# Second layer's output projection as fourteen half-size products instead of 128 full tile products

## The chip, the cores and the metric

The kernel runs on one core of one Trainium2 chip. The metric is the device time of one execution in microseconds. Three runs of the kernel before gave 971.11, 971.8 and 973.08 us, so the median is 971.8 us. The program is bound to one core, and the whole network (two layers) is one launch.

## The reference

512 tokens with 1024 features pass two layers. Each layer does: RMSNorm, a mixer, `h += RMSNorm(mixer output)`, and then a gated embedding (`ple`): `h += sigmoid(RMSNorm(h) W_g) * (p W_p)`. The mixer of layer 0 is a convolution and a gMLP; that of layer 1 is an mLSTM with 8 heads in 4 chunks of 128 tokens. Both mixers end in an output projection:

```
def mlstm_mixer(xn, w_in, b_if, mh_g, w_out):
    q, k, v, o, z, gif = jnp.split(xn @ w_in, ODD_SPLITS, axis=-1)
    ...                                   # hc: (512, 2048), 8 heads of 256
    y = hc * jax.nn.sigmoid(o) * jax.nn.silu(z)
    return y @ w_out                      # (512, 2048) @ (2048, 1024)

h = h + rmsnorm(y, post_g[i])
gate = jax.nn.sigmoid(rmsnorm(h, ple_g[i]) @ w_ple_gate[i])
h = h + gate * (p[i] @ w_ple[i])
```

All is float32. The change is about `y @ w_out` of layer 1.

## The kernel before

**Number format.** Every float32 operand of a large product is split in two float32r parts, `hi` (a copy by ScalarE) and `lo` (the original minus `hi`, by VectorE). A product is three matmuls: hi by hi, hi by lo, lo by hi. So each weight block costs ScalarE two activations and VectorE two subtractions of 128x1024, and each left operand is split likewise.

**Seven products for eight.** A product of two matrices cut in 2x2 blocks is done in seven block products instead of eight, with sums and differences of blocks on both sides (a Strassen scheme in Winograd's form). The products of a unit are named 1, 5, 6, 3, 2, 7, 4. Left sums are made by VectorE, right (weight) sums by a DMA that adds into SBUF (issued by GpSimd, `add_in`, `out_add`) or by VectorE (`s6_add`). One product has two passes `tp` (row tiles), each of 4 contraction tiles with 3 matmuls of 512 columns, so 12 matmuls a pass and 24 a product. The result gathers in PSUM banks: `a_of`, `b_of`, `c_of` are banks 0/1, 2/3, 4/5; small intermediate sums (`b_copy`, `s5_copy`, `c_make`) stand between products.

**Order of the work.** The input projections are 15 units (0 to 6 in layer 0, 7 to 14 in layer 1), each of seven products, in the list `STEPS`. Layer 0's output projection is already in this list, as 2 x 7 products (two halves `h` of the contraction) in the order `OUT_ORDER`. Each engine has its order written out by hand; semaphores join them. A weight block passes: SP loads it into one of five raw buffers (`raw7`: BX, BV, BA, BY, BZ), GpSimd may add another block to it there, ScalarE (`hi7`, L877) and VectorE (`lo7`, L1576) split it into a ring of three slots, TensorE uses it. The split of step g+2 is done during step g.

**Layer 1's output projection before.** It is a plain product (`odd_out` of TensorE, `token_tile` with L2331 to L2333): 2 column halves x 4 weight slots x 4 token tiles x 4 contraction tiles x 3 = 384 matmuls of 512 columns. The left operand y is split tile by tile (`y_high` L1037, `y_low` L1779), the first twelve tiles during the last input unit (unit 14), the last four (heads 6 and 7) during the projection. Weight slots are split by `hi` (L814) and `lo` (L1541).

**Heads 6 and 7.** The mLSTM work of the last two heads is cut in pieces which TensorE does between passes of the projection (`odd_end(i)` after pass i): intermediate states (`dstate` L2724), `scores` (L2733), `head_tile` (L2742, L2746), and the transposes of finished heads (`transpose_head` L2753), which ScalarE copies to y (`y_copy` L1377). Before, they stand at i = 0, 1, 2, 3, 5, 6, 7, 8 and 10.

**The end.** After the projection come the post norm (`residual` L1886, L1890), eight `ple` tiles with the transposes of the normed h between them (L2367), and the gate projection with its outputs. Layer 0 has the same with its own order (`PLE_ORDER[0]`).

Of the kernel before, what the change touches and what calls it, by code (L numbers as in the profile page):

```python
# [25 lines left out]
F32 = mybir.dt.float32  # L26
# [4 lines left out]
P = 128  # L31
SEQ = 512
# [32 lines left out]
OUT = 20  # L65
OUT_ORDER = ((0, 1), (1, 1), (0, 2), (0, 5), (1, 2), (1, 5), (0, 6), (1, 6), (0, 3), (1, 3), (0, 7), (1, 7),
# [6 lines left out]
OUT_PLACE = {what: place for place, users in OUT_PLACES.items() for what in users}  # L73
# [5 lines left out]
STEPS += [(u, p) for u in range(LEAD, UNITS) for p in order(u)]  # L79
STEP = {what: g for g, what in enumerate(STEPS)}  # L80
# [6 lines left out]
def out_left_count(h, p):  # L87
    return OUT_LEFTS.index((h, p)) + 1


def out_sum_count(h, p):
    return OUT_SUMS.index((h, p)) + 1
# [23 lines left out]
def source(u, p):  # L116

    if u >= OUT:
        return {5: (BZ, BV), 6: (BZ, BV), 4: (BZ, BV), 2: (BX, BX), 7: (BA, BX)}.get(p, (BA, BY))[u - OUT]
# [19 lines left out]
S_OUT = [0, 5]  # L139
S_PLE = [0, 13]  # L140
S_GATE = [1, 14]
SLOTS = 18
TAIL_ROWS = ROWS_IN + 8


N_OUT = [0, 16]
N_PLE = [0, 24]
N_GATE = [8, 32]


def raw_of(s):

    l = int(s >= S_OUT[1])
    r = (s - S_OUT[l]) % 2
    return r, (s - S_OUT[l]) // 2 + 1 + (3 - r if l else 0)


SLOT_RING = (1, 2)
SPARE_RING = 0


def slot_ring(s):
    return s % RING if s < S_OUT[1] else SLOT_RING[raw_of(s)[0]]


def slot_ends():
# [12 lines left out]
    def tail(l):  # L179
        for nb in range(2 * l):  # L180
            for _ in range(3):
                half()
            full(N_OUT[l] + 4 * nb + 4)
        full(N_PLE[l] + 8)
        for nb in range(2):
            half()
            full(N_GATE[l] + 4 * nb + 4)
# [18 lines left out]
def trunk(nc, x, p_in, slots, gif_w, g_rows, ln_rows, w_mix, b_mix, conv_w, gate_bias, head_g, out):  # L206
# [3 lines left out]
    def region(at, *spec):  # L210
# [53 lines left out]
    y0_hi, = region(L_AT, ("y0_hi", [P, 14, SEQ], F32R))  # L264
    y0_lo, = region(L_AT + 28 * KB, ("y0_lo", [P, 14, SEQ], F32R))
    y0_hi_end, = region(L_AT + 56 * KB, ("y0_hi_end", [P, 2, SEQ], F32R))
# [4 lines left out]
    p_hi_odd, p_odd, tanh_g, gated, g_post, g_ple = region(  # L271
        R_AT, ("p_hi_odd", [P, 2, SEQ], F32R), ("p_odd", [P, 2, SEQ], F32),
        ("tanh_g", [P, 2, SEQ], F32), ("gated", [P, 2, SEQ], F32), ("g_post", [P, D], F32),
        ("g_ple", [P, D], F32))
    p_lo_odd, y0_lo_end = region(W_AT + 8 * KB * SPARE_RING, ("p_lo_odd", [P, 2, SEQ], F32R),
# [2719 lines left out]
```

## Time and profile before

| what | value |
|---|---|
| median of three runs | 971.8 us |
| the profiled execution, own time | 971.55 us |
| its span (first to last instruction) | 969.8 us |
| TensorE busy | 961.0 us, 99% |
| VectorE busy | 670.7 us, 69% |
| ScalarE busy | 524.7 us, 54% |
| GpSimd busy | 102.3 us, 11% |
| mean DMA rate | 169 GB/s |

The page has busy time per engine, the span in 40 slices, the DMA queues, the chain of work that ended last, and the costliest groups of instructions by source line. A timeline row gives start, duration, engine, line, operation, output<-inputs, count, and in brackets how long the engine was idle before it and what released it. Matmuls are pipelined: their durations overlap, so their cost is the distance of their starts.

### The profile page before, as it was taken

How to read it: one execution, taken by the hardware profiler on the slowest of the kernel's cores; microseconds unless marked ns; L12 is line 12 of the kernel's file. 1: busy time of each engine (PE TensorE's matmuls, PEld its weight loads, DVE VectorE, ACT ScalarE, POOL GpSimd, SP SyncE). 2: the span in 40 equal slices, each digit the busy share in tenths (PEclk: the TensorE clock that was granted, in tenths of full speed). 3: DMA queues.
4: the chain of work that ended last, by engine and by line, in shares of the span. 5: the costliest groups of instructions: out<-in, count | busy, mean ns of one | idle time of the engine just before them, and what ended most of it. 6: DMA issues, size and time to landing. Idle time of an engine off the chain costs nothing.

```text
span 969.8 us, 12032 instructions
## 1 busy us (share of the span) xinstructions
PE 961.0 (99%) x4470; PEld 795.1 (82%) x4470; DVE 670.7 (69%) x885; ACT 524.7 (54%) x839; POOL 102.3 (11%) x136
## 2 busy tenths in 40 slices
PE   8999999999999999999999999999999999999998
PEld 7888888888877888887888888888888888888887
DVE  6767787786888687749797755775585676431835
ACT  6454554555455475636665656546654774441732
POOL 2020100101000113104010101010101000000500
PEclk9999999999999999999999999999999999999999
DMA  9655947649486993745956738392938163242122
GB/s 342 201 152 152 253 153 201 174 134 273 127 227 195 253 229 131 233 115 131 323 154 175 181 123 209 106 239 98 247 108 210 30 172 125 98 162 87 44 87 88
DMA packets 26268, 163.50 MB, mean 169 GB/s; under 512 B 3297, under 2 KB 3681, under 8 KB 8418
## 3 DMA queue, kind: packets, MB, share of 16 engines
q1 hardware_dynamic: 18722, 108.20, 29.3%
q0 software_dynamic: 7488, 54.53, 29.0%
q8 instruction: 36, 0.59, 0.2%
q14 instruction: 22, 0.18, 0.1%
HBM read 158.53 MB, written 4.19 MB: 168 GB/s over the span
## 4 chain that ended last, share of the span: by engine, by line
PE 96%; DVE 1%; ACT 1%; DMA 1%; issue 0%; POOL 0%; SPq 0%; DVEq 0%; ACTq 0%
PE bank L2425 18%; PE bank L2428 18%; PE bank L2427 18%; PE bank L2331 6%; PE bank L2333 6%; PE bank L2332 6%; PE bank L2458 3%; PE bank L2461 3%; PE bank L2460 3%; PE bank L2482 2%; PE bank L2484 2%; PE bank L2483 1%; PE bank L2742 1%; PE bank L2724 1%; PE bank L2746 1%; PE bank L2367 1%
## 5 line engine op out<-in xcount | busy, mean ns | idle before, releaser
L1576 DVE TENSOR_TENSOR w_lo<-raw,w_hi 128x1024 fp32r<-128x1024 f32 x230 | 271.3, 1221 | 151.4 <-ACT w_hi L877 150.8
L2425 PE MATMUL bank<-w_hi,l_hi 128*128 128x512 f32 x784 | 316.5, 404 | 0.5 <-DVE s L1694 0.4
L2428 PE MATMUL bank<-w_hi,l_lo 128*128 128x512 f32 x784 | 305.9, 390 | 0.0
L2427 PE MATMUL bank<-w_lo,l_hi 128*128 128x512 f32 x784 | 305.5, 390 | 0.0
L877 ACT ACTIVATE w_hi<-raw 128x1024 fp32r<-128x1024 f32 x230 | 230.7, 1054 | 106.4 <-DMA raw<-in_slots 53.9
L2425 PEld LDWEIGHTS bank<-w_hi,l_hi 128*128 128x128 f32 x784 | 147.3, 188 | 33.1 <-DVE s L1694 2.1
L2428 PEld LDWEIGHTS bank<-w_hi,l_lo 128*128 128x128 f32 x784 | 147.2, 188 | 31.3
L2427 PEld LDWEIGHTS bank<-w_lo,l_hi 128*128 128x128 f32 x784 | 147.3, 188 | 30.3 <-issue 1.0
L702 POOL DMA_DIRECT2D raw<-in_slots x44 | 39.2, 972 | 461.3 <-DVE w_lo L1576 434.9
L1541 DVE TENSOR_TENSOR w_lo<-raw,w_hi 128x1024 fp32r<-128x1024 f32 x36 | 42.4, 1220 | 55.9 <-ACT w_hi L814 55.9
L814 ACT ACTIVATE w_hi<-raw 128x1024 fp32r<-128x1024 f32 x36 | 36.2, 1059 | 65.3 <-PE bank L2333 62.8
L2331 PE MATMUL bank<-w_hi,x_hi 128*128 128x512 f32 x120 | 47.0, 391 | 0.0
L2333 PE MATMUL bank<-w_hi,x_lo 128*128 128x512 f32 x120 | 46.7, 389 | 0.0
L2332 PE MATMUL bank<-w_lo,x_hi 128*128 128x512 f32 x120 | 46.7, 389 | 0.0
L2331 PE MATMUL bank<-w_hi,y_hi 128*128 128x512 f32 x112 | 44.9, 401 | 0.2 <-DVE y_lo_end L1779 0.2
L2458 PE MATMUL bank<-w_hi,l_hi 128*128 128x512 f32 x112 | 45.1, 403 | 0.0
L2333 PE MATMUL bank<-w_hi,y_lo 128*128 128x512 f32 x112 | 43.7, 390 | 0.0
L2461 PE MATMUL bank<-w_hi,l_lo 128*128 128x512 f32 x112 | 43.7, 390 | 0.0
L2332 PE MATMUL bank<-w_lo,y_hi 128*128 128x512 f32 x112 | 43.6, 390 | 0.0
L2460 PE MATMUL bank<-w_lo,l_hi 128*128 128x512 f32 x112 | 43.6, 389 | 0.0
L686 POOL TENSOR_SCALAR rstds<-sums 128x1 f32<-128x1 f32 x20 | 19.2, 958 | 112.5 <-ACT square L825 112.1
L1583 DVE TENSOR_TENSOR raw<-raw 128x1024 f32<-128x1024 f32 x26 | 30.6, 1219 | 0.0
(263 smaller groups left out, 1339.1 us busy)
## 6 DMA issues: line engine op xcount, KB each, us to landing
raw<-in_slots SPq DMA_DIRECT2D x87, 1024.0 KB, 6.8
raw<-in_slots POOLq DMA_DIRECT2D x52, 1024.0 KB, 9.0
h<-in_x SPq DMA_DIRECT2D x8, 512.0 KB, 7.1
out<-h SPq DMA_DIRECT2D x4, 512.0 KB, 7.5
h<-out SPq DMA_DIRECT2D x4, 512.0 KB, 7.7
out<-h SPq DMA_DIRECT2D x7, 256.0 KB, 2.0
raw<-in_slots SPq DMA_DIRECT2D x2, 512.0 KB, 6.1
g_post<-in_g_rows SPq DMA_DIRECT2D x2, 512.0 KB, 6.0
```

The lines of the kernel that those rows point to most:

```text
L877: act.activation(w7_hi[:, ring(g), c], raw7[:, source(u, p), c], ACT.Copy).then_inc(w7_hi_ready, 1)
L1541: dve.tensor_tensor(w7_lo[:, slot_ring(s), c], raw[:, r, c], w7_hi[:, slot_ring(s), c].bitcast(F32), ALU.subtract).then_inc(lo_ready, 1)
L1576: dve.tensor_tensor(w7_lo[:, ring(g), c], raw7[:, source(*STEPS[g]), c], w7_hi[:, ring(g), c].bitcast(F32), ALU.subtract).then_inc(w7_lo_r ...
L2331: pe.matmul(bank[b][:, :], left_hi, w[0][:, k, c], start=(start and k == 0), stop=False)
L2332: pe.matmul(bank[b][:, :], left_hi, w[1][:, k, c], start=False, stop=False)
L2333: done = pe.matmul(bank[b][:, :], left_lo, w[0][:, k, c], start=False, stop=(stop and k == ks - 1))
L2425: pe.matmul(dst[:, :], left_hi, w7_hi[:, r, c], start=(first and k == 0), stop=False, skip_group_check=True)
L2427: pe.matmul(dst[:, :], left_hi, w7_lo[:, r, c], start=False, stop=False, skip_group_check=True)
L2428: done = pe.matmul(dst[:, :], left_lo, w7_hi[:, r, c], start=False, stop=(k == 3), skip_group_check=True)
L2458: pe.matmul(dst[:, :], left_hi, w7_hi[:, r, c], start=(first and k == 0), stop=False, skip_group_check=True)
L2460: pe.matmul(dst[:, :], left_hi, w7_lo[:, r, c], start=False, stop=False, skip_group_check=True)
L2461: done = pe.matmul(dst[:, :], left_lo, w7_hi[:, r, c], start=False, stop=(k == 3), skip_group_check=True)
```

## The change

Layer 1's output projection becomes 2 x 7 products in the list `STEPS`, as layer 0's is. Functions that served layer 0 alone (`out_product`, `out_high`, `out_low`, `out_fill`, `out_add`, the PSUM sums, `out_ends`) take the layer as an argument. The order of products and the places of the left operands are layer 1's own. During unit 14 the left operands (0,1), (0,2), (0,5), (0,6), (1,1), (0,4) are made, with four left sums (`odd_less`) between them. The head pieces move to i = 0, 1, 2, 3, 5 and 6. The load of h back from HBM is issued behind the sum for product (0,6). The end (`ple`, gate) takes layer 0's order.

```diff
+OUT_OF = (OUT, OUT + 10)
+ODD_ORDER = ((0, 1), (1, 1), (0, 5), (0, 2), (0, 6), (1, 5), (1, 2), (1, 6), (0, 3), (1, 3), (0, 7), (1, 7),
+             (0, 4), (1, 4))
+ODD_LEFTS = ((0, 1), (0, 2), (0, 5), (0, 6), (1, 1), (0, 4), (0, 7), (0, 3), (1, 5), (1, 2), (1, 6), (1, 3),
+             (1, 7), (1, 4))
+ODD_SUMS = ((0, 5), (0, 6), (0, 3), (0, 7), (1, 5), (1, 6), (1, 3), (1, 7))
+ODD_PLACES = {0: ((0, 1), (0, 3)), 1: ((0, 2), (1, 6)), 2: ((0, 5), (1, 2), (1, 4)), 3: ((0, 6), (1, 3)),
+              4: ((1, 1), (1, 5), (1, 7)), 5: ((0, 4),), 6: ((0, 7),)}
...
+ODD_STEP = len(STEPS)
+STEPS += [(OUT_OF[1] + h, p) for h, p in ODD_ORDER]
...
@@ SP: out_fill(l), v and a are BA and BV in layer 1
+            sp.wait_ge(w7_lo_ready, split_done(first, 1))
+            out_block(0, B22, a, out_x_in)
+            sp.wait_ge(w7_lo_ready, split_done(second, 1))
+            out_block(1, B22, BY, out_x_in)
+            sp.wait_ge(w7_lo_ready, split_done(first, 2))
             out_block(1, B21, BX, out_z_in)
-            sp.wait_ge(w7_lo_ready, split_done(OUT + 1, 2))
+            if l:
+                sp.wait_ge(out_s6_s4_in[0], 48)
+                sp.wait_ge(num_ready, 32)
+                sp.wait_ge(h_out, 16 * TILES)
+                for t in range(TILES):
+                    sp.dma_start(h[:, t], out[t * P:(t + 1) * P, :]).then_inc(h_in, 16)
+            sp.wait_ge(w7_lo_ready, split_done(second, 2))
             out_block(1, B12, BX, out_z_in)
@@ GpSimd
+        out_sum_5(1, 0)
+        out_sum_5(1, 1)
         head_root(6)
+        out_sum_6(1, 0)
         head_root(7)
+        out_sum_6(1, 1)
+        out_sum_7(1, 1)
+        out_sum_7(1, 0)
+        out_sum_4(1, 0)
+        out_sum_4(1, 1)
         post(1, 0)
@@ ScalarE: odd_out (out_ends follows it)
+            num_copy(6, 2, 6)
+            num_copy(6, 3, 7)
+            scale_rows(7, 4)
+            hi7(ODD_STEP + 2)
+            exponents(7)
+            out_high(1, 0, 7)
+            hi7(ODD_STEP + 3)
+            out_high(1, 0, 3)
+            num_copy(7, 0, LAST_NUM[0])
+            out_b_copy(1, 0)
+            out_b_copy(1, 1)
+            for n in range(1, TILES):
+                num_copy(7, n, LAST_NUM[n])
+            hi7(ODD_STEP + 4)
+            y_copy(6, 0, LAST_Y[0])
+            y_copy(6, 1, LAST_Y[1])
+            hi7(ODD_STEP + 5)
...
+            hi7(ODD_STEP + 7)
+            out_high(1, 1, 6)
+            out_s5_copy(1, 0)
+            out_s5_copy(1, 1)
+            out_high(1, 1, 3)
+            hi7(ODD_STEP + 8)
@@ VectorE, unit 14, behind lo7 of step k+2
+                    if k == 2:
+                        odd_less(0, 5)
+                        out_low(1, 0, 2)
+                    if k == 3:
+                        out_low(1, 0, 5)
+                        odd_less(0, 6)
+                    if k == 4:
+                        out_low(1, 0, 6)
+                        odd_less(0, 3)
+                    if k == 5:
+                        out_low(1, 1, 1)
+                        odd_less(0, 7)
@@ TensorE: odd_end
             if i == 1:
+                pe.wait_ge(num_used, 4 * 6 + 3)
+                scores(7, 6)
                 pe.wait_ge(c_free, 2 * LAST[1] + 2)
                 dstate(7, 0, 5)
-            if i == 2:
-                pe.wait_ge(num_used, 4 * 6 + 3)
-                scores(7, 6)
                 pe.wait_ge(num_used, 4 * 6 + 4)
                 dstate(7, 1, 7)
-            if i == 3:
+            if i == 2:
                 pe.wait_ge(state_ready, 3 * 7 + 1)
                 dstate(7, 2, 5)
-            if i == 5:
                 pe.wait_ge(isc_ready, 8)
                 pe.wait_ge(arg_ready, 32)
                 head_tile(7, 0, LAST_NUM[0])
+            if i == 3:
                 pe.wait_ge(state_ready, 3 * 7 + 2)
                 head_tile(7, 1, LAST_NUM[1])
...
+            if i == 5:
+                pe.wait_ge(num_used, 4 * 7 + 2)
+                transpose_head(6, 0, LAST_Y[0])
+                pe.wait_ge(num_used, 4 * 7 + 4)
+                transpose_head(6, 1, LAST_Y[1])
+            if i == 6:
                 for f in range(2):
-                    pe.wait_ge(num_used, 4 * 7 + 3 + f)
-                    transpose_head(7, f, LAST_Y[1][f])
+                    pe.wait_ge(y32_odd, 2 * 6 + f + 1)
+                    transpose_head(7, f, LAST_Y[f])
...
+        for o, (h_of, p) in enumerate(ODD_ORDER):
+            for tp in range(2):
+                out_product(1, h_of, p, tp)
+                odd_end(2 * o + tp)
         tail(1)
```

## Rows read from the trace of the kernel before

**Rows 1.** The page: span, TensorE's busy time, granted clock in 40 slices.
```profile
span 969.8 us, 12032 instructions
...
PE 961.0 (99%) x4470; PEld 795.1 (82%) x4470; DVE 670.7 (69%) x885; ACT 524.7 (54%) x839; POOL 102.3 (11%) x136
...
PEclk9999999999999999999999999999999999999999
```
**Rows 2.** The page: chain that ended last, shares of the span by engine.
```profile
PE 96%; DVE 1%; ACT 1%; DMA 1%; issue 0%; POOL 0%; SPq 0%; DVEq 0%; ACTq 0%
```
**Rows 3.** Timeline of TensorE, the old projection: start, duration, line, tiles.
```profile
810.82 0.39 PE L2331 MATMUL bank<-w_hi,y_hi 128*128 128x512 f32 x1
...
862.06 0.39 PE L2331 MATMUL bank<-w_hi,y_hi 128*128 128x512 f32 x1
...
907.62 0.39 PE L2331 MATMUL bank<-w_hi,p_hi_odd 128*128 128x512 f32 x1
```
**Rows 4.** Timeline of TensorE, after a head piece (L2724), and the one stall.
```profile
822.57 0.58 PE L2331 MATMUL bank<-w_hi,y_hi 128*128 128x512 f32 x1
822.99 0.40 PE L2332 MATMUL bank<-w_lo,y_hi 128*128 128x512 f32 x1
...
853.06 0.50 PE L2331 MATMUL bank<-w_hi,y_hi 128*128 128x512 f32 x1 [0.22 <-DVE y_lo_end L1779]
```
**Rows 5.** Timeline of TensorE, ple and gate begin: layer 0, then layer 1.
```profile
382.64 0.39 PE L2331 MATMUL bank<-w_hi,p_hi_even 128*128 128x512 f32 x1
...
396.58 0.47 PE L2331 MATMUL bank<-w_hi,x_hi 128*128 128x512 f32 x1
...
921.39 0.39 PE L2331 MATMUL bank<-w_hi,x_hi 128*128 128x512 f32 x1
```
**Rows 6.** Windows, busy us (instructions): layer 0's projection, unit 14's end, layer 1's projection.
```profile
302.30:382.60 80.30, 80.30 (x358) 65.45 (x357) 62.07 (x62) 46.81 (x67) 11.92 (x13) 1.00 0.73 199
796.00:811.00 15.00, 15.00 (x68) 12.44 (x67) 13.71 (x22) 9.30 (x18) 0.00 (x0) 1.00 0.63 203
811.00:907.60 96.60, 96.38 (x437) 79.85 (x437) 36.55 (x59) 33.65 (x65) 6.35 (x9) 1.00 0.29 106
```
**Rows 7.** Timeline of VectorE at unit 14's end; timeline of TensorE there, last row.
```profile
799.97 2.36 DVE L1541 TENSOR_TENSOR w_lo<-raw,w_hi 128x1024 fp32r<-128x1024 f32 x2 [0.38 <-ACT w_hi L814]
...
804.44 1.28 DVE L1779 TENSOR_TENSOR y_lo<-y,y_hi 128x512 fp32r<-128x512 f32 x2
805.64 0.68 DVE L1694 TENSOR_TENSOR s<-s,bank 128x512 f32<-128x512 f32 x1
...
807.87 0.58 PE L2425 MATMUL bank<-w_hi,l_hi 128*128 128x512 f32 x1
```
**Rows 8.** Timeline of VectorE, a left sum of layer 0's projection.
```profile
327.52 1.22 DVE L1769 TENSOR_TENSOR y<-y 128x1024 f32<-128x1024 f32 x1
```
**Rows 9.** Timeline of VectorE and of ScalarE, head 7 and the copy of y.
```profile
822.96 0.48 DVE L2078 SCALAR_TENSOR_TENSOR state<-state,sc,bank 128x257 f32<-128x257 f32 x1 [3.60 <-PE bank L2724]
823.36 0.69 DVE L2069 SCALAR_TENSOR_TENSOR expo<-bank,expo 128x512 f32<-128x512 f32 x1
...
816.27 0.48 ACT L1335 ACTIVATE expo<-bank 128x384 f32<-128x384 f32 x1
...
840.20 2.01 ACT L814 ACTIVATE w_hi<-raw 128x1024 fp32r<-128x1024 f32 x2 [1.91 <-PE bank L2333]
842.11 0.67 ACT L1377 ACTIVATE y<-bank,head_g_sb 128x512 f32<-128x512 f32 x1
```
**Rows 10.** L737 and L702, GpSimd's adding DMAs: issues at 313.6, 326.8 to 327.4, 504.3 to 504.8.
```profile
DMA to landing us min/median/max: 7.9/7.9/7.9
...
DMA to landing us min/median/max: 11.6/14.1/16.6
...
DMA to landing us min/median/max: 10.6/14.4/18.3
```
**Rows 11.** L651, SP's four loads of h back from HBM in layer 1.
```profile
DMA to landing us min/median/max: 5.7/7.7/9.0
```

More of the change, by code:

```diff
@@ L179, in tail @@
     def tail(l):
[L180 to L183, printed above, removed]
         full(N_PLE[l] + 8)
@@ L587, in out_block, with out_fill @@
-        def out_block(h, blk, b, landed):
-            sp.dma_start(raw7[:, b], slots[out_row(h, blk)]).then_inc(landed, 16)
-        def out_fill():
-            u = LAST[0]
+            row(g_post_of[l], g_rows[3 * l + 1:3 * l + 2, :], tail_in)
+            row(g_ple_of[l], g_rows[3 * l + 2:3 * l + 3, :], tail_in)
+        def out_fill(l):
+            u = LAST[l]
+            first, second = OUT_OF[l], OUT_OF[l] + 1
+            v, a = ((BV, BA), (BA, BV))[l]
+            def out_block(h, blk, b, landed):
+                sp.dma_start(raw7[:, b], slots[out_row(l, h, blk)]).then_inc(landed, 16)
@@ new lines, in out_fill @@
+            out_block(1, B12, BX, out_z_in)
+            if l:
+                sp.wait_ge(yt_ready, 16)
+                p_load(1)
+            else:
+                sp.wait_ge(ybt_ready, 8)
+                p_load(0)
+                for t in range(TILES):
+                    sp.dma_start(h[:, t], x[t * P:(t + 1) * P, :]).then_inc(h_in, 16)
+                sp.dma_start(g_raw[:, :, :], gif_w).then_inc(gw_in, 16)
+            sp.wait_ge(tail_in, 48 * l + 16)
+            sp.wait_ge(w7_lo_ready, split_done(second, 3))
@@ L624, in _ @@
+            load(S_PLE[l], wait=False)
+            sp.wait_ge(w7_lo_ready, split_done(first, 7))
+            rows_load(l)
+            sp.wait_ge(w7_lo_ready, split_done(first, 4))
+            load(S_PLE[l] + 1, wait=False)
         fill(0)
-        out_fill()
+        out_fill(0)
         load(2)
@@ L1521, in odd_oz @@
                 if u == LAST[1] and k >= 1:
-                    y_high(2 * k - 2)
-                    y_high(2 * k - 1)
+                    out_high(1, *ODD_LEFTS[k - 1])
         odd_oz(0)
@@ new lines, in odd_out @@
+        def odd_out():
+            for tp in range(2):
+                z_gate(3, 2 + tp)
+                o_gate(3, 2 + tp)
+            head_norm(6)
+            scaled_args(7, 4)
+            make_state(7, 0, 5)
+            make_state(7, 1, 7)
+            probs(7, 6)
+            lo7(ODD_STEP + 2)
+            make_state(7, 2, 5)
+            head_scale(6)
+            out_low(1, 0, 7)
+            lo7(ODD_STEP + 3)
+            out_low(1, 0, 3)
+            head_norm(7)
+            head_scale(7)
+            lo7(ODD_STEP + 4)
+            lo7(ODD_STEP + 5)
+            odd_less(1, 5)
+            out_low(1, 1, 5)
+            lo7(ODD_STEP + 6)
+            odd_less(1, 6)
+            out_low(1, 1, 2)
+            odd_less(1, 3)
+            odd_less(1, 7)
+            lo7(ODD_STEP + 7)
+            out_low(1, 1, 6)
+            out_low(1, 1, 3)
+            lo7(ODD_STEP + 8)
+            out_low(1, 1, 7)
+            out_c_make(1, 0)
@@ L2887, in _ @@
         first_transpose(1, 3)
-        for g in range(TURN + 1, len(STEPS)):
+        for g in range(TURN + 1, ODD_STEP):
             u, p = STEPS[g]
```

747 lines of the change are left out of this document (297 added, 450 removed).

## Prediction, on record before the changed kernel was run

> **What bounds the kernel now.** I read the page first: TensorE is busy 961.0 of 969.8 us at full granted clock in every slice [rows 1]. A busy engine need not be the bound, so I went to the chain of waits, where 96% of the span are TensorE's own instructions one behind the other [rows 2]. Then I read the distance of matmul starts, since durations overlap. Between 862.06 and 907.62 stand 201 matmuls of 512 columns (67 triples, no head piece among them): 45.56 / 201 = 0.2267 us each, though each row says 0.39 [rows 3]. In the old projection TensorE waits once for VectorE: the matmul at 853.06 shows 0.22 us of wait, and its start is 0.61 behind the one before, 0.38 more than the pace [rows 4]. VectorE is at rest most of this stage, 36.55 of 96.60 us, but just before it, from 796 to 811, it is busy 13.71 of 15 us [rows 6]. So a matmul taken away is worth its pace, if VectorE, ScalarE and the DMAs keep their deadlines in an order where they get more to do.
>
> The Trainium skill (TensorE: Matmul & The Clock Gate, Back-to-back issue gap) gives a sustained spacing of about 131 ns for N=512. This trace has 227 ns, so it doesn't agree; by the page's figure the 48 matmuls below would be worth 6.3 us and the time would be 965.5.
>
> **The change part by part.** All sums are against the profiled execution: 971.55 us with a span of 969.8, so 1.75 lie around the span; it stands 0.25 below the median of 971.8. I take the difference from the span and subtract it from the median.
>
> 1. *The matmuls.* Old: 2 x 4 x 4 x 4 x 3 = 384. New: 14 products x 2 passes x 4 x 3 = 336. 48 go, 48 x 0.2267 = 10.88 us, all on the path.
>
> 2. *The head pieces.* The old stage runs from 810.82 to 907.62 = 96.80 us [rows 3], less 384 x 0.2267 = 87.05 leaves 9.75 for pieces, their switches and the stall. The new pieces are the same instructions, so their work stays. They stand at six places instead of nine; the return from a piece shows one start distance of 0.42 instead of 0.23 [rows 4], so 3 x 0.19 = 0.57 go (bounds 0 and 1.1). The stall of 0.38 belongs to the last tiles' `y_low`, which is gone (bounds 0 and 0.38). Together -0.95, which leaves 8.8 us of pieces.
>
> 3. *Left operands in unit 14.* The six `out_high`/`out_low` pairs take the place of six pairs of `y_high`/`y_low` tiles of the same number of elements (1.22 for one 128x1024 operation against 1.28 for two tiles [rows 7, 8]): zero. New are four left sums of 1.13 to 1.2 us each, start to start. The first two and the third meet idle time of VectorE, except the third's last part: the split of 799.97 had waited 0.38 for ScalarE, so it slips by about 0.7. With the fourth sum the subtraction L1694 at 805.64, which `product(14,4)` pass 1 waits for, moves by 0.7 + 1.13 to 1.2, less what one 128x1024 subtraction saves over two tiles, to about 807.4 and ends near 808.1. TensorE wants it at 807.87 [rows 7]. Cost 0.3 us; bounds 0 (a little more slack than the rows show) and 1.3 (the four sums' 4.6 us less the idle that they find, by the first row of that group and the 1.3 us free in the window).
>
> 4. *Head 7, now tighter.* `scores` and the second `dstate` come one pass (2.7 us) earlier. Before, VectorE sat idle 3.60 us for that `dstate`, and the probabilities were made at 823.36 to 824.05 [rows 9]. Now VectorE reaches them at about 820.7, done by 821.4, and TensorE asks for them at i = 2, after its third pass, near 822.9 (811.1 + 3 x 2.72 + about 3.6 of pieces). ScalarE has a weight split of 2.0 us in front of the exponentials, between 816.7 (the end of the row at 816.27) and 818.7; the arguments are ready only about 819, so it is hidden, if the sum for (1,5) has landed by then. Its block's load is issued one step ahead of the split at 799.97, near 796; with 7.7 us as for the h loads [rows 11] and 7.9 for the sum [rows 10] it lands near 812. Margin about 4.7 us. Cost zero; uncovered, each us late is a us.
>
> 5. *Three sums with deadlines.* The weight sums (`out_add`) of layer 1 are new: eight adding DMAs of 1 MB. Alone one lands in 7.9 us, two or three together or beside the h and p loads of layer 0 took 11.6 to 16.6 us, the worst of the whole run 18.3 [rows 10]. Five have a step or more to spare. The three others:
>  - (0,6): VectorE ends the split of (0,5) at 821.4 + 2.3 = 823.7, so the add is issued at 824.0. ScalarE stands at this split (2.01) and has the two copies of y of head 6 (0.67 each) behind it [rows 9], and TensorE's transposes of head 7 at i = 6 wait for these. TensorE gets there at 811.1 + 7 x 2.72 + 7.95 of pieces = 838.1. 838.1 - 3.3 - 824.0 = 10.8, a little more for the second transpose: 11 us allowed.
>  - (1,6): the split of (1,5) ends near 840; TensorE starts step 7 at 858.1; in between stand split 2.0, high 1.05, low 1.2. 13.8 us allowed.
>  - (0,7): the split of (0,3) ends near 858; step 10 starts at 874.4; split 3.4 for both engines. 12.7 us allowed. The sum for (1,7), issued about 5 us earlier, is in flight, which I take as 10.7.
>  The h loads are issued when the sum for (0,6) has landed, at about 832, and land in 5.7 to 9.0 us [rows 11], by 841, as the sum for (1,6) starts. SP has nothing urgent queued behind: (1,2)'s split and B12 come at 846. They are needed at the post norm, near 886. Cost zero in the likeliest case; bounds 0 and the rival below. I put 0.1 into the sum.
>
> 6. *VectorE and ScalarE in the stage.* Layer 0's stage of the same form has 62.07 of 80.30 us of VectorE and 46.81 of ScalarE, and TensorE is never short there [rows 6]. Layer 1's new stage on VectorE: 12 splits x 2.27, 8 `out_low` and 4 sums x 1.13, some 11 for heads and gates, 8 for the end = 60 of 85 us. Hidden by TensorE's 85 us.
>
> 7. *The end.* With layer 0's order `ple` lasts from 382.64 to 396.58 = 13.94 us; layer 1's old order took 907.62 to 921.39 = 13.77 [rows 3, 5]. +0.17. Everything after is the same work; the three-slot ring gives it more room, not less. Layer 0's own code keeps its order and its addresses: zero.
>
> Sum: -10.88 - 0.95 + 0.3 + 0.1 + 0.17 = -11.26, and I give back 0.15 for what I can't see, so -11.1: span 958.7, time 971.8 - 11.1 = **960.7 us**. The stage ends near 811.1 + 76.2 + 8.8 = 896.1 instead of 907.6.
>
> **The rivals.** *B, a sum lands late.* If one of the three takes 16.6 us, TensorE stalls 5.6, 2.8 or 3.9 us: 963.5 to 966.3, say 964.8. For it: layer 0 shows such landings in this very pattern, and the h loads are now close to (1,6). Against: there three adds and five loads lay together within 10 us, here one or two, and TensorE did not stall even so. The mechanism is that both queues' packets share the same engines (the window is at 199 GB/s [rows 6]). The Trainium skill (DMA: Bandwidth & Descriptors, Queues, rings and completion order) has each engine go round-robin between its queues a packet at a time; the rows of 7.9 against 16.6 agree with that.
>
> *C, the head chain on VectorE and ScalarE.* One of the hand-made orders in parts 3 and 4 is too tight: the fourth left sum in front of L1694, or the probabilities behind a late split. Price 1 to 4 us, 963.0 as its time. For it: 13.71 of 15 us busy [rows 6]. Against: the idle time found above.
>
> *D, slower: all sums late.* Each delayed sum delays the split that lets the next be issued, so the stalls add up: with a landing L for all three the stage loses 3L - 37.5. The gain of 11.1 is gone at L = 16.2 us; at 18.3 [rows 10] it is 17.4 us, 978.1. Place: TensorE before i = 6, (1,6) and (0,7). Against: it needs the worst landing three times in a row with a near-empty queue.
>
> *E, no change.* The matmuls go, but something else has the stage's old length. Nothing in the rows has it: VectorE needs 60 us, and 16 blocks of 1 MB with 2 MB of h have 85 us to pass. 971.8.
>
> **How the numbers follow.** Chances: A (forecast) 0.74, B 0.13, C 0.07, D 0.04, E 0.02. A's own range is 959.0 to 962.0: below, all switches and the stall and no cost in 3 and 7 (-10.88 - 1.1 - 0.38 = -12.4), and 0.4 for the scatter of a median; above, nothing from part 2 but 0.38, 1.3 in part 3, 0.17 in part 7. The range to hold 8 in 10 goes on to C and B's middle: 959.0 to 965.0. What a measurement of this kernel can tell from no change is about 0.2%, 1.9 us. Faster by more than that: A + B + C = 0.94. Within: E, 0.02. Slower: D, 0.04.
>
> **What would show it.** In the changed trace the projection's first matmul starts near 811.1 and the first `ple` matmul near 896; 336 matmuls at 0.227 us; TensorE has no wait over 0.5 us there. The first start of `product(14,4)` pass 1 within 0.5 us of 807.87. The adding DMAs for (0,6), (1,6), (0,7) land in 8, 8 to 9 and about 11 us. The prediction is wrong if TensorE waits more than 1 us for a split or for y, at i = 2, i = 6, step 7 or step 10; if the pace differs from 0.227; or if the stretch after the projection gets longer by more than 0.3 us.

## The result and the profile after

| | changed kernel | kernel before |
|---|---|---|
| median | 962.12 us (961.45 to 962.74, 4 runs) | 971.53 us (971.11 to 973.08, 4 runs) |
| ratio | 0.9896 (95% interval 0.9884 to 0.9907) | 1 |

9.4 us were gained where 11.1 had been forecast. The profiled execution took 962.74 us with a span of 961.0, which is 8.8 us less span than before (969.8).

The page of the changed kernel: span, busy time, granted clock, and the chain that ended last.

```profile
span 961.0 us, 11999 instructions
...
PE 950.7 (99%) x4422; PEld 785.7 (82%) x4422; DVE 702.1 (73%) x907; ACT 542.6 (56%) x853; POOL 109.4 (11%) x144
...
PEclk9999999999999999999999999999999999999999
...
PE 87%; DVE 5%; DMA 5%; ACT 2%; issue 1%; POOL 0%; DVEq 0%; ACTq 0%
```

TensorE has 48 instructions fewer and its clock is whole, but the chain is no longer 96% TensorE [rows 2]: it now also leads through VectorE, ScalarE and a DMA. The timeline of TensorE says where. A pair names a product: (14,3) is product 3 of unit 14, (0,6) is product 6 of the projection's first half. The rows are the first matmul of product (14,3) pass 1 (my marker, since it follows a head piece in every version), the one before and the first of (14,4) pass 0, the first of pass 1, the projection, `ple` and the gate.

```profile
788.14 0.58 PE L2418 MATMUL bank<-w_hi,l_hi 128*128 128x512 f32 x1
...
803.51 0.39 PE L2421 MATMUL bank<-w_hi,l_lo 128*128 128x512 f32 x1
805.58 0.50 PE L2418 MATMUL bank<-w_hi,l_hi 128*128 128x512 f32 x1 [1.68 <-DVE s L1674]
...
810.04 0.50 PE L2418 MATMUL bank<-w_hi,l_hi 128*128 128x512 f32 x1
...
812.87 0.39 PE L2453 MATMUL bank<-w_hi,l_hi 128*128 128x512 f32 x1
...
898.50 0.39 PE L2324 MATMUL bank<-w_hi,p_hi 128*128 128x512 f32 x1
...
912.42 0.47 PE L2324 MATMUL bank<-w_hi,x_hi 128*128 128x512 f32 x1
```

In the kernel before the marker is this row:

```profile
788.43 0.58 PE L2425 MATMUL bank<-w_hi,l_hi 128*128 128x512 f32 x1
```

With [rows 3, 5] for before, the difference of spans splits into five stretches:

| stretch | before | after | difference |
|---|---|---|---|
| span's start to the marker | 788.43 | 788.14 | -0.29 |
| marker to the projection (end of unit 14) | 22.39 | 24.73 | **+2.34** |
| the projection | 96.80 | 85.63 | **-11.17** |
| `ple` | 13.77 | 13.92 | +0.15 |
| gate and end | 48.41 | 48.58 | +0.17 |

So the projection gave 11.17 of the 11.73 us forecast for it (10.88 + 0.95 - 0.1), and the end of unit 14, where a loss of 0.3 us was forecast, took back a fifth of that. Before pass 0 of the last product TensorE's starts are 2.07 apart instead of 0.23. It waits for VectorE (L1674, `s5_make`). Here are VectorE and then ScalarE at that time, in brackets what each had waited for:

```profile
802.57 2.36 DVE L1556 TENSOR_TENSOR w_lo<-raw,w_hi 128x1024 fp32r<-128x1024 f32 x2 [2.19 <-ACT w_hi L888]
804.84 0.68 DVE L1674 TENSOR_TENSOR s<-s,bank 128x512 f32<-128x512 f32 x1
...
809.30 0.68 DVE L1674 TENSOR_TENSOR s<-s,bank 128x512 f32<-128x512 f32 x1
```

```profile
801.40 2.01 ACT L888 ACTIVATE w_hi<-raw 128x1024 fp32r<-128x1024 f32 x2 [2.78 <-DMA raw<-in_slots]
```

`s5_make` stands in VectorE's order behind the split of (0,1)'s block, that split stands behind ScalarE's, and ScalarE waited 2.78 us for a load. The load is not the one of (0,1)'s own block. `hi7` waits for `out_x_in >= 64 * l + 32`, the count after the B11 blocks of both halves, and the second half's came last. Its issue on SP and the adding DMA for (0,5) on GpSimd, with their landings:

```profile
L577 SPq DMA_DIRECT2D raw<-in_slots x1: 328/328/328, 789.3 to 789.3; - x1
...
  ACT w_hi L888: 2.8, 1
...
DMA to landing us min/median/max: 12.1/12.1/12.1
```

```profile
L728 POOL DMA_DIRECT2D raw<-in_slots x1: 888/888/888, 788.6 to 788.6; - x1
...
DMA to landing us min/median/max: 12.6/12.6/12.6
```

The load landed at 801.4, the instant at which ScalarE started. The block before it on SP's queue had landed in 5.4 us. A second, smaller part of the 2.34 (0.50) lies at pass 1: from pass 0 to the projection 7.29 us passed instead of 6.79.

The busy table of the end of unit 14 and of the projection (PE, PEld, DVE, ACT, POOL, granted clock, DMA share, GB/s) answers to [rows 6]:

```profile
795.80:810.80 15.00, 13.19 (x57) 10.38 (x56) 12.81 (x17) 7.12 (x14) 0.87 (x1) 1.00 0.75 203
812.87:898.50 85.63, 85.60 (x390) 71.03 (x389) 66.11 (x85) 53.75 (x88) 14.60 (x18) 1.00 0.66 182
```

VectorE works 66 us in the projection instead of 37 (60 were forecast), and all of it but 0.27 us is hidden behind TensorE's work. The adding DMAs there landed in 8.9 us for (0,6), in 8.0 for (1,6), and the last three, (0,7), (0,4) and (1,4), in flight together, like this:

```profile
L728 POOL DMA_DIRECT2D raw<-in_slots x3: 862/875/1230, 860.4 to 862.6; - x3
...
DMA to landing us min/median/max: 8.1/14.4/20.3
```

None of these three is what TensorE feels. The 0.27 us are lost at the first matmul of (0,4): it starts at 887.50, 0.42 behind the start before it (887.08), with an uneven distance of 0.31 after it. By the code it waits for `out_d_make` (L1896). These are VectorE's rows:

```profile
884.43 2.36 DVE L1556 TENSOR_TENSOR w_lo<-raw,w_hi 128x1024 fp32r<-128x1024 f32 x2 [4.22 <-DMA g_ple_odd<-in_g_rows]
886.71 1.49 DVE L1896 TENSOR_TENSOR bank<-s,bank 128x512 f32<-128x512 f32 x2
```

L1896 stands behind the split of (1,4), and VectorE began this split only when a plain load had landed, that of the row `g_ple` (512 KB, issued at 872.4, 12.0 us), for which its order has a wait just in front of the split. The sum for (1,4) had landed at 882.9 (862.6 + 20.3), and ScalarE needs about 1 us for the first half of its split, so the sum alone would have let VectorE start near 883.9, half a microsecond sooner. No run tests this by itself; all twelve profiles with the new projection have VectorE released by this load there, and TensorE's distance lies between 0.36 and 0.70. That is the spread of the projection's length in the table below (e5 apart).

### The profile page after: what moved, and what is told of

It reads as the page before. It is cut to its first block, busy times and chain, and to the rows that moved or that the text cites. A ratio compares the mean times of both kernels' runs of the same rounds, so it can differ in the third digit from the quotient of the medians.

```text
span 961.0 us, 11999 instructions
## 1 busy us (share of the span) xinstructions
PE 950.7 (99%) x4422; PEld 785.7 (82%) x4422; DVE 702.1 (73%) x907; ACT 542.6 (56%) x853; POOL 109.4 (11%) x144
## 4 chain that ended last, share of the span: by engine, by line
PE 87%; DVE 5%; DMA 5%; ACT 2%; issue 1%; POOL 0%; DVEq 0%; ACTq 0%
PE bank L2418 15%; PE bank L2421 15%; PE bank L2420 15%; PE bank L2453 5%; PE bank L2456 5%; PE bank L2455 5%; DMA raw<-in_slots 4%; PE bank L2324 3%; PE bank L2326 3%; PE bank L2325 3%; DVE w_lo L1556 3%; PE bank L2479 2%; PE bank L2477 2%; PE bank L2478 2%; PE bank L2699 1%
## 5 line engine op out<-in xcount | busy, mean ns | idle before, releaser
L1556 DVE TENSOR_TENSOR w_lo<-raw,w_hi 128x1024 fp32r<-128x1024 f32 x258 | 304.4, 1221 | 161.3 <-ACT w_hi L888 153.9
L888 ACT ACTIVATE w_hi<-raw 128x1024 fp32r<-128x1024 f32 x258 | 258.7, 1054 | 127.5 <-DMA raw<-in_slots 73.2
L2418 PE MATMUL bank<-w_hi,l_hi 128*128 128x512 f32 x784 | 316.7, 404 | 2.2 <-DVE s L1674 1.8
L2421 PE MATMUL bank<-w_hi,l_lo 128*128 128x512 f32 x784 | 305.9, 390 | 0.0
L2420 PE MATMUL bank<-w_lo,l_hi 128*128 128x512 f32 x784 | 305.6, 390 | 0.0
L2418 PEld LDWEIGHTS bank<-w_hi,l_hi 128*128 128x128 f32 x784 | 147.2, 188 | 36.0 <-DVE s L1674 5.0
L2421 PEld LDWEIGHTS bank<-w_hi,l_lo 128*128 128x128 f32 x784 | 147.2, 188 | 31.3
L2420 PEld LDWEIGHTS bank<-w_lo,l_hi 128*128 128x128 f32 x784 | 147.4, 188 | 30.2 <-issue 1.0
L2453 PE MATMUL bank<-w_hi,l_hi 128*128 128x512 f32 x224 | 89.7, 400 | 0.0
L2456 PE MATMUL bank<-w_hi,l_lo 128*128 128x512 f32 x224 | 87.3, 390 | 0.0
L2455 PE MATMUL bank<-w_lo,l_hi 128*128 128x512 f32 x224 | 87.2, 389 | 0.0
L2453 PEld LDWEIGHTS bank<-w_hi,l_hi 128*128 128x128 f32 x224 | 42.1, 188 | 10.1 <-issue 1.4
L2455 PEld LDWEIGHTS bank<-w_lo,l_hi 128*128 128x128 f32 x224 | 42.1, 188 | 9.2 <-issue 0.7
L2456 PEld LDWEIGHTS bank<-w_hi,l_lo 128*128 128x128 f32 x224 | 42.0, 188 | 8.8
L1768 DVE TENSOR_TENSOR l_lo<-y,l_hi 128x1024 fp32r<-128x1024 f32 x26 | 31.5, 1220 | 1.9 <-ACT l_hi L1042 1.9
L835 ACT ACTIVATE square<-h 128x512 f32<-128x512 f32 (+1 forms) x28 | 19.4, 694 | 20.1 <-DVE h L1880 14.3
L1521 DVE TENSOR_TENSOR w_lo<-raw,w_hi 128x1024 fp32r<-128x1024 f32 x20 | 23.5, 1219 | 9.6 <-ACT w_hi L824 9.6
```

Of the source, the lines that this page charges most:

```text
L888: act.activation(w7_hi[:, ring(g), c], raw7[:, source(u, p), c], ACT.Copy).then_inc(w7_hi_ready, 1)
L1556: dve.tensor_tensor(w7_lo[:, ring(g), c], raw7[:, source(*STEPS[g]), c], w7_hi[:, ring(g), c].bitcast(F32), ALU.subtract).then_inc(w7_lo_r ...
L2418: pe.matmul(dst[:, :], left_hi, w7_hi[:, r, c], start=(first and k == 0), stop=False, skip_group_check=True)
L2420: pe.matmul(dst[:, :], left_hi, w7_lo[:, r, c], start=False, stop=False, skip_group_check=True)
L2421: done = pe.matmul(dst[:, :], left_lo, w7_hi[:, r, c], start=False, stop=(k == 3), skip_group_check=True)
L2453: pe.matmul(dst[:, :], left_hi, w7_hi[:, r, c], start=(first and k == 0), stop=False, skip_group_check=True)
```

## The experiments

Timed runs of one kernel scatter over 2 to 4 us here (before: 970.65 to 974.65 in 10 runs), in part for a reason told under "hardware" below. So each verdict rests on two stretches of the profile, marker to projection (22.39 before) and the projection itself, and the medians stand beside them. "Lead" is how far ahead of the load of the second half's B11 the adding DMA for (0,5) was issued (us; negative: behind it).

| run | median us | ratio to before, 95% | to projection | projection | lead | load landed in |
|---|---|---|---|---|---|---|
| changed kernel | 962.12 | 0.9884 to 0.9907 | 24.73 | 85.63 | 0.7 | 12.1 |
| e1 own semaphore | 962.45 | 0.9879 to 0.9916 | 22.45 | 85.84 | 0.2 | 6.1 |
| e2 sum behind load | 962.37 | 0.9880 to 0.9917 | 22.45 | 85.55 | add last | 4.7 |
| e3 two left sums late | 963.02 | 0.9879 to 0.9923 | 22.39 | 85.64 | 0.2 | 5.7 |
| e4 e1 and e3 | 961.97 | 0.9873 to 0.9914 | 22.39 | 85.77 | 0.1 | 6.0 |
| e5 fifth product fourth | 967.45 | 0.9937 to 0.9965 | 24.42 | 89.47 | 0.6 | 11.8 |
| e6 h beside the sum | 962.45 | 0.9887 to 0.9916 | 24.47 | 85.57 | 0.6 | 11.9 |
| e7 load held back | 962.44 | 0.9882 to 0.9914 | 24.27 | 85.74 | 2.4 | 9.4 |
| e8 e7 with e1's semaphore | 962.13 | 0.9869 to 0.9901 | 22.45 | 85.68 | 2.2 | 10.0 |
| c changed kernel again | 963.63 | 0.9892 to 0.9924 | 24.81 | 85.91 | 0.7 | 12.2 |
| e9 before, 48 matmuls less | 963.37 | 0.9883 to 0.9917 | 22.39 | 86.58 | | |
| e10 both layers | 961.62 | 0.9875 to 0.9903 | 22.39 | 85.71 | -0.2 | 5.6 |
| e11 e3 again | 962.33 | 0.9882 to 0.9922 | 22.39 | 85.84 | 0.1 | 5.8 |

**e1, a semaphore of its own for that load (layer 1).**

```diff
-            out_block(1, B11, BY, out_x_in)
+            out_block(1, B11, BY, out_y_in if l else out_x_in)
@@ ScalarE, hi7
-                if p == 1:
-                    act.wait_ge(out_x_in, 64 * l + 32)
+                if p == 1 and l:
+                    act.wait_ge(out_y_in if h_of else out_x_in, 16 if h_of else 80)
```

> Theory (the split of product (0,1) waits for a block that it does not use): in layer 1 the load of the second half's first block gets a semaphore of its own, so ScalarE's split for product (0,1) no longer waits 2.78 us for it. TensorE's wait of 1.68 us before product(14,4) is gone, the start distance there falls from 2.07 to under 0.5 us; a wait of up to 0.5 us may come up at its second pass. Time 1.4 to 1.9 us under the changed kernel's 962.1, so 960.4, ratio to before 0.988. Rival (VectorE is too full there, the left sums hold up the subtraction): at least 1 us of the wait stays and the time is 961.5 to 962.

**e2, the adding DMA for (0,5) waits until the load has landed.**

```diff
+        pool.wait_ge(out_x_in, 96)
         out_sum_5(1, 0)
```

> Theory (the load lands late since GpSimd's adding DMA for product (0,5), issued 0.7 us before it, shares the engines): here that adding DMA is held back until the load has landed, all else as in the changed kernel. The load issued near 789.3 lands in 5 to 7.5 us instead of 12.1, ScalarE's split for (0,1) has no DMA wait, TensorE's wait before product(14,4) is gone: time 960.4. Both sums of the fifth products then land by about 814, before ScalarE needs them at 818. Rival (the load is late for another reason, such as HBM or the queue): it still lands in 10 us or more, and the time stays at 962 or rises, as the sums are later too.

**e3, the left sums for (0,3) and (0,7) behind the last left operand of unit 14.**

```diff
                     if k == 6:
                         out_low(1, 0, 4)
+                        odd_less(0, 3)
+                        odd_less(0, 7)
```

> The left sums (0,3) and (0,7) are made at the end of unit 14, behind both subtractions that product(14,4) waits for; all else as in the changed kernel. Theory (a DMA wait of ScalarE is the cause): the wait of TensorE before pass 0 stays at 1.7 us within 0.2, since VectorE sat idle 2.19 us before its late split; only the start of pass 1 moves, by 0.5 us at most. Time 961.6 to 962.1. Rival (VectorE too full): the wait before pass 0 falls by 1 us or more, time 960.5.

**e4, e1 and e3 together.**

> Own semaphore for the load and the two left sums late, together. Theory: no wait of TensorE over 0.1 us at either pass of product(14,4); time 0.2 to 0.5 us under that of the own semaphore alone, 960.0 to 960.2. If VectorE's load counts for nothing: the same as with the semaphore alone. If the late sums delay head 6's gates: a new wait of TensorE at the first head pieces and a time at or above 960.4.

In all four the stretch to the projection is back at 22.4 us. The times did not follow: e1, e2 and e4 were to take 960.0 to 960.4 us and took 962.0 to 962.5, about what the changed kernel took, and e3 took 963.0 where 961.6 to 962.1 were expected. The stretches also proved less than I had hoped: in e3, which by its expectation was to keep the stall, where the semaphore and both queues' code are those of the changed kernel, the stall is gone too. That is the outcome which e3's expectation gives to the rival (VectorE too full), but the landings say otherwise. In e1, e3 and e4 the add led by 0.1 to 0.2 us only, and there the load took 5.7 to 6.1 us and the add 12. The marker, the projection's start and the load of e3:

```profile
790.31 0.58 PE L2418 MATMUL bank<-w_hi,l_hi 128*128 128x512 f32 x1
...
812.70 0.39 PE L2453 MATMUL bank<-w_hi,l_hi 128*128 128x512 f32 x1
```

```profile
L577 SPq DMA_DIRECT2D raw<-in_slots x1: 328/328/328, 791.4 to 791.4; - x1
...
DMA to landing us min/median/max: 5.7/5.7/5.7
```

So e1, e3 and e4 don't separate the shared semaphore, the left sums and the order of the two DMAs; e2 adds only that with the load alone (4.7 us) there is no stall either. For the semaphore the load had to be late on purpose.

**e7, the load held back until the arguments of head 6 are ready; e8, the same with e1's semaphore.**

```diff
+            if l:
+                sp.wait_ge(arg_ready, 28)
             out_block(1, B11, BY, out_x_in)
```

> The changed kernel, with the layer-1 load of the second half's B11 block held back until the arguments of head 6 are ready, about 1.6 us later, so that the adding DMA for (0,5) is always well ahead of it. Theory (whichever of the two 1 MB transfers is first in the engines' queues is done first, and ScalarE's split of (0,1) waits for this load, though it doesn't use it): the load lands about 10 to 12 us after its issue, 1.5 to 2 us later than in the changed kernel or the same, TensorE waits 1.7 to 3.5 us before pass 0 of the last product of unit 14, and the stretch from product (14,3) pass 1 to the projection is 25 to 27 us instead of 22.4. Rival (the load takes its 5.7 to 6 us wherever it is issued): it lands in 6 us, the stretch is 22.4 to 22.8 us.

> The kernel with the load held back in the same way, but with a semaphore of its own for this load, so that the split of (0,1) waits for its own block alone. Theory (the shared semaphore is what turns the late load into a stall): the load is as late as with the shared one, but TensorE does not wait, and the stretch from product (14,3) pass 1 to the projection is 22.4 to 22.8 us; the time is 2 to 4 us below that of the kernel with the shared semaphore. Rival (the late transfer itself is the cause, through the adding DMA or VectorE's left sums): the stretch is as long as with the shared semaphore.

The load's rows, e7 first and then e8:

```profile
L577 SPq DMA_DIRECT2D raw<-in_slots x1: 328/328/328, 794.0 to 794.0; - x1
...
DMA to landing us min/median/max: 9.4/9.4/9.4
```

```profile
L578 SPq DMA_DIRECT2D raw<-in_slots x1: 328/328/328, 792.6 to 792.6; - x1
...
DMA to landing us min/median/max: 10.0/10.0/10.0
```

In both the load is late, 12.8 us behind the marker in each (803.4 - 790.61 and 802.6 - 789.77), later than e1's 7.3 and near the changed kernel's 13.3. TensorE stands 1.23 us in e7 and not at all in e8: 24.27 against 22.45. The two kernels differ in the semaphore alone, so the pair shows that it is the shared semaphore which turns a late load into the stall, and with the four left sums in place in e8 it also shows that VectorE is not short there. Three misses: the load took 9.4 us in e7 and not 10 to 12; its stretch of 24.27 and wait of 1.23 lie below the 25 to 27 and 1.7 to 3.5 expected; and in time the pair differs by 0.3 us where 2 to 4 were expected (e7 from 960.68 to 964.89, e8 from 960.46 to 962.55).

**e5, the fifth product fourth.**

```diff
-ODD_ORDER = ((0, 1), (1, 1), (0, 5), (0, 2), (0, 6), ...
+ODD_ORDER = ((0, 1), (1, 1), (0, 2), (0, 5), (0, 6), ...
```

> The changed kernel with the first half's products 2 and 5 exchanged in layer 1's order, so that the fifth product stands fourth. The sum for (0,6) is issued behind the split of (0,5), which is now one step (5.4 us) later, while the product that wants it stays fifth. Theory (the sum's deadline is what this place of the fifth product buys): the sum needs about 9 us as before (8.9 in the changed kernel), its allowed landing shrinks from about 11 to 5.6 us, so TensorE waits 3 to 4 us at step 4 or at the transposes of i = 6, and the piece from the projection's first matmul to the first ple matmul grows from 85.5 to 88.5 to 89.5 us; time 965 to 967. Rival (a sum has slack of its own in ScalarE's and VectorE's free time, the place is worth nothing): that stretch stays at 85.5 to 86.

The projection is as expected (89.47, of 88.5 to 89.5), the time 0.45 above its range, and part of the loss is a surcharge that I had not reckoned with. TensorE at the transposes of i = 6, and the busy table just behind:

```profile
839.58 0.39 PE L2456 MATMUL bank<-w_hi,l_lo 128*128 128x512 f32 x1
841.98 1.69 PE L2710 MATMUL bank<-ident,num 128*128 128x128 f32 x8 [2.01 <-ACT y L1379]
...
843.90 0.63 PE L2455 MATMUL bank<-w_lo,l_hi 128*128 128x512 f32 x1
844.32 0.63 PE L2456 MATMUL bank<-w_hi,l_lo 128*128 128x512 f32 x1
844.75 0.63 PE L2453 MATMUL bank<-w_hi,l_hi 128*128 128x512 f32 x1
```

```profile
842.00:846.00 4.00, 4.00 (x15) 3.33 (x16) 3.31 (x4) 3.55 (x5) 0.00 (x0) 0.57 0.99 405
```

The sum landed in 8.0 us where 5.6 were allowed, TensorE's starts are 2.40 apart (2.17 lost; 8.0 - 5.6 = 2.4), and then the granted clock is 0.57, so the lower of its two levels (1.2 instead of 2.4 GHz) for most of 4 us: matmuls 0.42 apart instead of 0.23. That costs the other 1.7 of the 3.84 us by which the projection is longer. Putting the fifth product third instead of fourth is worth these 3.8 us of the projection and, against the changed kernel's two medians, 3.8 to 5.3 us of time.

**e6, the loads of h one wait earlier.**

```diff
             if l:
-                sp.wait_ge(out_s6_s4_in[0], 48)
                 sp.wait_ge(num_ready, 32)
```

> The changed kernel with one wait less on the queue that loads h: the four loads no longer wait for the sum of (0,6), so they are issued some 3 us earlier, beside it. Theory (two streams share the DMA engines, so the sum is what pays): the sum for (0,6) lands in 11 to 13 us instead of 8.9; ScalarE splits it later by 2 to 4 us, and as about 2 us are free TensorE waits 0 to 2 us before the transposes of i = 6; projection 85.5 to 87.5 us, time 962 to 964. Rival (h loads are small beside the sum and the free time covers them): the sum lands below 10 us and the projection stays at 85.5.

The rival was right. The sum for (0,6) landed in 7.9 us (8.9 in the changed kernel), the projection stayed at 85.57, and it was h that paid: 6.3 to 8.3 us instead of 3.7 to 7.4. Counted from the marker h came 3.5 us earlier, but at 832.5 it was still 5.7 us behind the sum's issue (826.8), so the two overlapped by some 2 us only; a longer overlap was not tested. Loading h behind the sum buys nothing here.

**e9, the first term by itself.**

```diff
-            for k in range(ks):
+            for k in range(ks - (left is None and k0 in (4, 8))):
```

> The kernel before, with 48 of the 384 matmuls of its output projection left out: every tile of the second and third weight slot takes three contraction tiles instead of four, so a part of the contraction is missing in the result. Nothing else is changed: same splits, same loads, same pieces. Theory (a matmul taken away is worth its pace): the projection is 96.8 - 48 x 0.2273 = 85.9 us, the time 10.9 us below that of the kernel before, 961.3 us where that has 972.2. Rival (VectorE, ScalarE or the weight loads come in sight once the passes are shorter): 1 to 3 us of the 10.9 are missing, with a wait of TensorE for a split.

The projection is 86.58 us, 10.22 less; the time is 9.1 us below that of the kernel before run beside it (963.37 against 972.43), where 10.9 were expected. The missing 0.7 of the projection is at the one stall that [rows 4] shows, now deeper:

```profile
851.20 0.50 PE L2331 MATMUL bank<-w_hi,y_hi 128*128 128x512 f32 x1 [0.90 <-DVE y_lo_end L1779]
```

Pieces and stalls taken out, 336 matmuls take 76.35 us in e9 and in the changed kernel alike, 0.2272 each.

**c, the changed kernel again, and e10, the version that the experiments point to** (e4 with the semaphore in layer 0 as well), beside e9 on the same chip.

```diff
-            out_block(1, B11, BY, out_y_in if l else out_x_in)
+            out_block(1, B11, BY, out_y_in)
@@ ScalarE, hi7
+                if p == 1 and h_of:
+                    act.wait_ge(out_y_in, 16 * l + 16)
+                elif p == 1:
+                    act.wait_ge(out_x_in, 48 * l + 16)
```

> The changed kernel once more, beside the two below, on the same chip. In its first profile the load of the second half's B11 was issued 0.7 us behind the adding DMA and landed in 12.1 us, and TensorE stood 1.7 us before the last product of unit 14. Theory (a race of less than a microsecond between two queues, the same code can fall either way): a new profile shows one of two cases, the stretch from product (14,3) pass 1 to the projection at 24.3 to 24.8 us with the load at about 12 us, or at 22.4 us with the load at about 6 us, and nothing between. Rival (the stall belongs to the code, the experiments without it differ by their edits): 24.7 us again. Time 962 us in both.

> The version that the experiments point to: the load of the second half's B11 has a semaphore of its own in both layers, and the left sums for (0,3) and (0,7) stand behind the last left operand of unit 14. Theory: no wait of TensorE for VectorE's left operands at the end of unit 14 (stretch 22.4 us), projection 85.6 to 85.8, so its profile has 2.3 us less there than the first one of the changed kernel; layer 0 loses its wait of 0.17 us too. If the changed kernel falls into its stall in every run, the median is 2 us below it, about 960.2; if only in some, 0 to 1 us below it, which five rounds can hardly tell. Rival (something else sets the time there): the stretch stays above 23 us.

c has the stall again, which its expectation gives to the rival (the stall belongs to the code), with nearly the first profile's numbers:

```profile
808.51 0.50 PE L2418 MATMUL bank<-w_hi,l_hi 128*128 128x512 f32 x1 [1.76 <-DVE s L1674]
```

e10 runs 961.50 to 961.77 us and c 962.12 to 965.97, run side by side, so here the ranges don't touch and the medians are 2.0 apart; the stretch to the projection is 2.4 us shorter. The times alone don't prove e10 the better kernel: the changed kernel's first four runs (961.45 to 962.74) reach into e10's range, and the intervals of the two ratios overlap. All five runs of c show a mean granted clock of 0.998 and two of e10's four show 1.000, so part of the 2.0 is the clock (below).

The record also has the span and the clock of each single run, and among the runs with a clock of 1.000 the stall can be seen. Six such runs of e1, e2, e3, e8 and e11, whose profiles have no stall, span 958.5 to 958.8 us; the changed kernel's one spans 961.0 and e6's two 960.7 and 961.7. The gap is near the 2.3 us of the stall. It is not clean: e7, with the stall in its profile, has 958.5, 960.2 and 961.0, and e10, without it, 959.6 and 960.0.

**e11, e3 once more.** Three programs with the changed kernel's code up to here (the changed kernel twice, e5, e6) had the add 0.6 to 0.7 ahead, and e3 had not. Was that chance?

> The kernel with the left sums for (0,3) and (0,7) behind the last left operand of unit 14, once more. Its queues are those of the changed kernel, whose two profiles both have the adding DMA 0.7 us ahead of the load and the load at 12.1 to 12.2 us; the one profile of this kernel had it 0.2 us ahead and the load at 5.7. Theory (the load of the block before lands in 5.4 to 6.0 us by chance, and that decides, so a program may fall either way): the add can be 0.6 to 0.7 us ahead this time, with the load at about 12 us; then TensorE waits 0.5 to 1.7 us before the last product's pass 0 (the moved sums take 0 to 1.2 us off it). Rival (it belongs to the program): 0.2 us ahead again, the load at 5.7 to 6.1 us, stretch from product (14,3) pass 1 to the projection 22.4 us.

The rival again: 0.1 ahead, load 5.8, stretch 22.39. So in the programs looked at twice the outcome came out the same twice. The add waits for the block before on SP's queue, which landed in 5.4 to 5.5 us in the four profiles with the long landing and in 5.7 to 6.3 in all others; as far as these profiles show, that half microsecond makes the difference. Why it falls one way in one program and the other way in another is open. e7 has it at 5.9, though its code up to that point is the changed kernel's.

## Why the prediction was right, and where not

The time was forecast at 960.7 us and came out at 962.12. That lies inside the range of 959.0 to 965.0 only because the range goes on to the rivals' middle: the forecast's own part of it ends at 962.0. Two of the signs that were named beforehand failed. The first start of `product(14,4)` pass 1 was to lie within 0.5 us of 807.87 and came at 810.04; and the stretch after the projection, which was not to grow by more than 0.3 us, went from 62.18 (969.8 - 907.62) to 62.50, so by 0.32, at the limit. The pace, and no wait over 0.5 us in the projection, held.

**Step 1** was right: 48 x 0.2267 = 10.88 forecast. By the stretches of steady matmuls it was 87.27 - 76.35 = 10.92.

**Step 2** failed in its first term. It took 0.57 off for three head pieces fewer. Taken as distances of starts less the pace, the same work costs the same merged or apart. The intermediate state alone, and `scores` with a state, cost 0.44 and 1.32 before, and in one place 1.76 after; the transposes 1.77 before and after. In the rows below, from the last matmul before the piece (820.08) to the second one behind it (822.30) are 2.22 us, two paces and 1.76: one return of 0.42 instead of two, but the piece itself is longer by the other.

```profile
820.08 0.39 PE L2456 MATMUL bank<-w_hi,l_lo 128*128 128x512 f32 x1
820.31 1.05 PE L2690 MATMUL bank<-qk 128*128 128x128 f32 x8
821.20 1.03 PE L2681 MATMUL bank<-v_odd,kw 128*128 128x257 f32 x4
821.88 0.58 PE L2453 MATMUL bank<-w_hi,l_hi 128*128 128x512 f32 x1
822.30 0.39 PE L2455 MATMUL bank<-w_lo,l_hi 128*128 128x512 f32 x1
```

All pieces and stalls together came to 9.53 before and 9.28 after. The old stall (0.49 with its tail) went, and 0.27 before (0,4) came. So the step gave 0.25 instead of 0.95, and the projection took 85.6 instead of 85.0.

**Step 3** is the one that cost the rest: 0.3 forecast, bounds 0 to 1.3, and 2.34 measured. The four left sums in front of L1694, for which the 0.3 stood, cost less: with the load's wait out of the way (e1, e8) all four cost 0.06 us. What failed was the list of deadlines. I followed VectorE's order and the adding DMAs with a near deadline, and passed over a plain load. It is (1,1)'s block, and I gave it no deadline before (1,1)'s split, while a wait count ties it to (0,1)'s, one split earlier. Counting which semaphore value each split waits for, in the code, would have shown it. The load of `g_ple` in front of (1,4)'s split is a second plain load that the list passed over; it cost 0.27 us.

**Steps 4 to 6** held: no wait at i = 2, i = 6, step 7 or step 10. The three sums with deadlines landed in 8.9, 8.0 and 8.1 us where 8, 8 to 9 and about 11 were forecast. Of the two behind them, 14.4 and 20.3, the second is beyond the worst row of before (18.3); neither is what TensorE waited for. The 0.1 put into the sum for step 5 was not needed there. Step 6 had VectorE at 60 us where it works 66, without consequence. **Step 7** was 0.15 for 0.17; the gate and the end are 0.17 longer, unforecast.

Added up: -10.92 - 0.25 + 2.34 + 0.15 + 0.17 - 0.29 (before the marker) = -8.8, the difference of the spans. Of the rivals, B had the right kind of cause (two 1 MB transfers at once, one of them late, a wait at its split) but in the wrong place and for another transfer, C the right place with the wrong cause; neither came about as written. The margins from which B and D were priced are borne out once: e5 takes 5.4 us from that of (0,6), which leaves 5.6, and the sum's 8.0 us stop TensorE for 2.17. That such stalls add up from sum to sum, as D has it, no run shows. The 0.15 given back for the unseen was too little for a stage boundary at which loads, adding DMAs and the orders of several engines all change. e11's profiled execution had a span of 958.7 us, exactly the forecast's; that is luck in part, as its projection took 85.84 us and not 85.0.

## What to carry to other kernels

A semaphore that counts several transfers ties each reader to the last of them: list, for every split or product, the value it waits for and which transfers that includes, plain loads too, before reckoning deadlines. Give each transfer that may be overtaken its own semaphore; it cost nothing in the stretches measured here (e8, e10), and the wait of the reader that does not need the transfer is gone, whichever way a race of half a microsecond falls. Small pieces of work merged into fewer places are not cheaper by the switches saved, unless rows show the merged form: here they were not. And where a stall costs more than it lasts, look at the granted clock behind it.

## What the runs showed of the hardware

**Two 1 MB transfers issued close together.** A plain load from SP and an adding DMA from GpSimd: with the add 0.6 to 0.7 us ahead both took 11.8 to 12.7 us and landed within 0.2 us of each other (the changed kernel twice, e5, e6). With the add only 0.1 to 0.2 us ahead the load took 5.7 to 6.1 and the add 12.0 to 12.3. With it 2.2 to 2.4 ahead, 9.4 to 10.0 for the load and 8.5 to 9.4 for the add. The Trainium skill (DMA: Bandwidth & Descriptors, Queues, rings and completion order) has each engine go round-robin between its queues a packet at a time. The equal landings of the first case agree with that; the load of the second, 5.7 to 6.1 us beside 4.7 alone (e2), does not look like an equal share from the start. No run here shows where the difference arises. One order that changes sign between the two cases is that in which the issuing instructions end: the add's lasts 0.89 us on GpSimd and the load's 0.33 on SP, so with a lead of 0.7 the add's ends first (789.46 against 789.6 in the changed kernel), and with 0.2 the load's does. Whether that decides was not tested.

**The lower clock behind a wait of 2 us.** At the start of layer 1 TensorE waits 2.05 us for VectorE in every profile, before and after. In e1 to e4, e7 to e9 and c the clock fell to the lower level behind it; in the others it did not. The same stretch in c and in the changed kernel:

```profile
446.00:448.00 2.00, 2.00 (x7) 1.52 (x6) 1.97 (x3) 2.00 (x7) 0.65 (x2) 0.50 0.36 66
```

```profile
446.00:448.00 2.00, 2.00 (x14) 1.69 (x12) 2.00 (x4) 2.00 (x5) 1.45 (x3) 1.00 0.75 209
```

The marker at the end of unit 14 stands at 787.98 to 789.11 where it did not fall and at 789.54 to 791.32 where it did. In c's row 0.50 is the lower level (1.2 GHz), in the other 1.00 the upper (2.4 GHz). The mean granted clock from 440 to 450 is 0.83 in these eight and 1.00 in the other six profiles, so 1.7 of 10 us were lost; the rest of the marker's scatter, some 1 us, I can't place. Nor is the clock all of the scatter of the times: the kernel before, in its runs with a mean clock of 1.000, spans 968.9 to 971.8 us. No edit explains either: the changed kernel's own code shows both outcomes of the clock. Together they cover the 2.3 us of the stall in the medians. The Trainium skill (TensorE: Matmul & The Clock Gate, HAM oscillation — how this bites in real kernels) describes such a fall behind a wait for a DMA; here the wait was for another engine, and the same wait in the same program did it in one execution and not in the next (c against the changed kernel).
